# Two transformer blocks on one core: the convolution's mean one gate slab earlier, expert rows and results on ScalarE's DMA queue, half of the final sums on TensorE

## What is computed

```python
# convolution branch: mean and variance over the 512 channels of a token
u = silu(layernorm(u, ln_g, ln_b)); conv_out = u @ pw_w
logf = log_sigmoid(f_logit + fox_bf)          # forget gates, summed over time into the fox scores
merged = sigmoid(gate_c) * conv_out + sigmoid(gate_a) * attn_out
x = x + merged @ w_out
...
# experts: two per token, then the last norm
y = sum over the two chosen experts of weight * ((silu(h @ w_gate) * (h @ w_up)) @ w_down)
out = rmsnorm(x + y, norm_final_g)
```

## Time and profile before

| | |
|---|---|
| median of 3 runs | 1669.45 us (1664.61 to 1675.3) |
| profiled execution | 1670.66 us; its span 1668.9 us, 1.8 us lie around it |
| PE / PEld busy | 1468.2 us (88%) / 1156.5 us (69%) |
| DVE / ACT / POOL busy | 776.2 us (47%) / 603.4 us (36%) / 501.9 us (30%) |
| mean granted TensorE clock | 0.909 of 2.4 GHz |
| chain that ended last | PE 79%, DVE 9%, ACT 4%, issue 4%, POOL 3%, DMA 2% |

### The profile page before, as it was taken

How to read it: one execution, slowest core, us unless ns; L and a number is a source line. 1 busy time by engine, 2 the same in 40 slices (tenths; PEclk the granted TensorE clock), 3 DMA queues, 4 the chain that set the end, 5 groups by cost and what they waited for, 6 DMA issues and landing times.

```text
span 1668.9 us, 17895 instructions
## 1 busy us (share of the span) xinstructions
PE 1468.2 (88%) x7024; PEld 1156.5 (69%) x7024; DVE 776.2 (47%) x1174; ACT 603.4 (36%) x932; POOL 501.9 (30%) x202
## 2 busy tenths in 40 slices
PE   6999897799879999999968989699999889299991
PEld 4877776578668888888847867465678767277770
DVE  3358357853353533333050793334352235466654
ACT  4443244332352322223142123433333434255552
POOL 2352022000235655556334433311133520201102
PEclk9999598756899999999978999799999999599996
DMA  5232102000144544444403323100122411779964
GB/s 197 82 114 89 51 26 101 1 2 1 42 139 136 151 142 141 137 148 152 151 26 101 99 91 101 51 26 26 51 76 101 177 53 65 313 269 422 417 252 177
DMA packets 97798, 204.28 MB, mean 122 GB/s; under 512 B 6672, under 2 KB 56080, under 8 KB 91056
## 3 DMA queue, kind: packets, MB, share of 16 engines
q1 hardware_dynamic: 90512, 176.87, 31.2%
q0 software_dynamic: 7200, 26.22, 4.0%
HBM read 168.99 MB, written 34.08 MB: 122 GB/s over the span
## 4 chain that ended last, share of the span: by engine, by line
PE 79%; DVE 9%; ACT 4%; issue 4%; POOL 3%; DMA 2%; POOLq 0%; SPq 0%; DVEq 0%; ACTq 0%
PE bank L496 19%; PE bank L498 18%; PE bank L497 18%; PE bank L2618 4%; PE bank L740 3%; PE bank L759 2%; DVE rw_work L1478 2%; PE bank L750 2%; PE bank L1144 2%; PE bank L742 1%; POOL wlo L433 1%; DVE rw_beta L1476 1%; ACT whi L425 1%; PE bank L666 1%; PE bank L2585 1%
## 5 line engine op out<-in xcount | busy, mean ns | idle before, releaser
L433 POOL TENSOR_TENSOR wlo<-raw,whi 128x2048 fp32r<-128x2048 f32 (+1 forms) x84 | 382.8, 4558 | 731.9 <-ACT whi L425 731.9
L496 PE MATMUL bank<-alo,whi 128*128 128x512 f32 (+1 forms) x728 | 291.2, 400 | 18.4 <-issue 7.6
L497 PE MATMUL bank<-ahi,whi 128*128 128x512 f32 (+1 forms) x728 | 286.9, 394 | 0.0
L498 PE MATMUL bank<-ahi,wlo 128*128 128x512 f32 (+1 forms) x728 | 286.8, 394 | 0.0
L425 ACT ACTIVATE whi<-raw 128x2048 fp32r<-128x2048 f32 (+1 forms) x84 | 159.0, 1893 | 309.6 <-PE bank L498 309.6
L496 PEld LDWEIGHTS bank<-alo,whi 128*128 128x128 f32 (+1 forms) x728 | 138.7, 191 | 51.8 <-issue 14.1
L498 PEld LDWEIGHTS bank<-ahi,wlo 128*128 128x128 f32 (+1 forms) x728 | 138.6, 190 | 29.9
L497 PEld LDWEIGHTS bank<-ahi,whi 128*128 128x128 f32 (+1 forms) x728 | 138.8, 191 | 29.3 <-issue 0.7
L1889 DVE TENSOR_TENSOR ffn_relu<-ffn_relu 128x512 f32<-128x512 f32 x32 | 97.7, 3053 | 107.3 <-ACT ffn_relu L1869 107.3
L496 PE MATMUL bank<-wlo,ffn_hi 128*128 128x512 f32 x256 | 100.4, 392 | 1.3 <-POOL wlo L433 1.3
L497 PE MATMUL bank<-whi,ffn_hi 128*128 128x512 f32 x256 | 100.3, 392 | 0.0
(11 more groups left out here) (415 smaller groups left out, 2635.0 us busy)
## 6 DMA issues: line engine op xcount, KB each, us to landing
raw<-in_w_in_dram SPq DMA_DIRECT2D x18, 1024.0 KB, 5.3
expert_gate_up<-in_expert_w_gate_dram SPq DMA_DIRECT2D x17, 1024.0 KB, 10.8
expert_gate_up<-in_expert_w_up_dram SPq DMA_DIRECT2D x17, 1024.0 KB, 13.8
expert_down<-in_expert_w_down_dram SPq DMA_DIRECT2D x17, 1024.0 KB, 7.9
raw<-in_w_ffn_up_dram SPq DMA_DIRECT2D x16, 1024.0 KB, 6.7
raw<-in_w_ffn_down_dram SPq DMA_DIRECT2D x16, 1024.0 KB, 5.6
raw<-in_w_in_first_dram SPq DMA_DIRECT2D x12, 1024.0 KB, 5.4
expert_rows_dram<-zero_rows SPq DMA_DIRECT2D x23, 512.0 KB, 7.5
```

The source lines that it names most:

```text
L433: nc.gpsimd.tensor_tensor(wlo[:, n % SPLIT, 0:k * c], raw[:, n % RAW, 0:k * c], whi[:, n % SPLIT, 0:k * c].bitcast(F32), ALU.subtract).the ...
L496: nc.tensor.matmul(acc, sh, ml, start=first and i == 0, stop=False)
L497: nc.tensor.matmul(acc, sh, mh, start=False, stop=False)
L498: ins = nc.tensor.matmul(acc, sl, mh, start=False, stop=last and end)
```

## The change

It has four parts.

1. In the convolution, the mean follows the second gate slab instead of the third and the variance the third instead of the fourth. ACT's list moves with it: square root, SiLU and high parts (`act_conv_end`) stand ahead of the fourth slab's sigmoids. POOL's list has the remainder of ga.0.0 ahead of the four `u_lo`. The constant `minus8` is made by ACT instead of DVE, and DVE finishes the forget gates ahead of the reciprocal.
2. The experts' rows are read, and their results stored, by DMAs that ACT issues from its own list; POOL issues only the scatter and the gather.
3. DVE makes 8 diagonal matrices of the routing weights and then waits until POOL has issued the whole scatter (`rows_issued`, a small memset behind the 8 indirect DMAs) before it makes the first weight remainders (L2816).
4. The left 512 columns of the last sums are made on PE: the identity times `x`, plus the two diagonal matrices times the gathered rows. DVE sums the right half. ACT squares each half by itself, and DVE scales each half by itself, the left one from PSUM.

```diff
@@ pe_phase3 @@
-                for at, name, made, src in ((2, "conv_mean", conv_made, conv), (3, "conv_var", conv_dev2, conv_sq)):
+                for at, name, made, src in ((1, "conv_mean", conv_made, conv), (2, "conv_var", conv_dev2, conv_sq)):
...
-            pe.wait_ge(forget_dve, 5)
+            pe.wait_ge(forget_dve, 4)
@@ act_phase3 @@
+            nc.scalar.activation(minus8[:, :, :], ident[0:NHEAD, 0:NHEAD].unsqueeze(2).broadcast_to([NHEAD, NHEAD, P]), ACT.Copy,
+                                 scale=-float(HD) ** 0.5).then_inc(forget_act, 1)
             for i, n in enumerate(GATE_C):
-                if i == 3:
+                if i == 2:
...
+                if i == 3:
+                    act_conv_end(act)
                 for j in range(2):
                     acc = banks.take(act, f"{n}/{j}")
                     nc.scalar.activation(merged[:, 2 * i + j, :], acc[:, :], ACT.Sigmoid).then_inc(gate_sig, 1)
                 make_hi(act, act_slab, slab_no[n] + 1 + SPLIT)
@@ pool_phase3 @@
-            make_lo(pool, pool_slab, slab_no[GATE_C[3]] + 1)
+            make_lo(pool, pool_slab, slab_no[GATE_A[0]] + 1)
@@ pe_phase5 @@
+            pe_sum(pe)
+        SUM_BANKS = TURN_BANKS + GATE_UP_BANKS
+        LEFT, RIGHT = slice(0, 512), slice(512, 1024)
+        def pe_sum(pe):
+            for t in range(NT):
+                nc.tensor.matmul(SUM_BANKS[t][:, :], ident, x[:, t, LEFT], start=True, stop=False)
+            for t in range(NT):
+                pe.wait_ge(y_gathered[t], 16 * TOPK)
+                for k in range(TOPK):
+                    ins = nc.tensor.matmul(SUM_BANKS[t][:, :], diag_w[:, k, t, :], y_pair[:, t, k, LEFT], start=False, stop=k == TOPK - 1)
+                ins.then_inc(halves_summed, 1)
@@ act_phase5 @@
             act_w_hi(act, 1, 0)
+            act.wait_ge(rows_placed, 16 * NT * TOPK)
+            for i in range(2):
+                act_tile_in(act, i)
             act_x_hi(act, 0)
-            act.wait_ge(rows_placed, 16 * NT * TOPK)
+            act_tile_in(act, 2)
             for i in range(SURE):
                 if 0 < i < SURE - 1:
                     act_w_hi(act, i + 1, 0)
                 if i > 1:
                     act_y(act, i - 2)
+                    act_tile_out(act, i - 2)
                 if i:
                     act_hidden_t(act, i - 1)
                 if i < SURE - 1:
                     act_x_hi(act, i + 1)
+                    if i + 3 < SURE:
+                        act_tile_in(act, i + 3)
                     act_w_hi(act, i + 1, 1)
                 act_silu(act, i)
...
+        def act_final(act, t):
+            def after(n):
+                act.wait_ge(final_squares, 3 * t + n)
+            act.wait_ge(halves_summed, t + 1)
+            if t >= 2:
+                after(-3)
+            nc.scalar.activation(final_sq[:, t % 2, LEFT], SUM_BANKS[t][:, :], ACT.Square, accum_out=sums5[:, t:t + 1]).then_inc(final_squares, 1)
+            after(1)
+            nc.scalar.activation(sums5[:, 12 + t:13 + t], sums5[:, t:t + 1], ACT.Identity, scale=1.0 / D,
+                                 bias=const("eps")[:, 0:1]).then_inc(final_squares, 1)
+            act.wait_ge(y_sums, 2 * t + 2)
+            nc.scalar.activation(final_sq[:, t % 2, RIGHT], x[:, t, RIGHT], ACT.Square, accum_out=sums5[:, 16 + t:17 + t]).then_inc(final_squares, 1)
+            after(3)
+            nc.scalar.activation(sums5[:, 4 + t:5 + t], sums5[:, 16 + t:17 + t], ACT.Sqrt, scale=1.0 / D,
+                                 bias=sums5[:, 12 + t:13 + t]).then_inc(final_root, 1)
@@ dve_phase5 @@
             dve_route(dve, steps)
+            for k in range(TOPK):
+                for t in range(NT):
+                    steps.link(nc.vector.tensor_scalar(diag_w[:, k, t, :], ident, weight[:, k, t:t + 1], None, ALU.mult))
+            dve.wait_ge(rows_issued, 1)
             for c in range(CHUNKS):
                 dve_w_lo(dve, 0, c)
@@ dve_sum, dve_final @@
-                    nc.vector.scalar_tensor_tensor(out=x[:, t, :], in0=y_pair[:, t, k, :], scalar=weight[:, k, t:t + 1], in1=x[:, t, :],
-                                                   op0=ALU.mult, op1=ALU.add).then_inc(y_sums, 1)
+                    nc.vector.scalar_tensor_tensor(out=x[:, t, RIGHT], in0=y_pair[:, t, k, RIGHT], scalar=weight[:, k, t:t + 1],
+                                                   in1=x[:, t, RIGHT], op0=ALU.mult, op1=ALU.add).then_inc(y_sums, 1)
...
+                for part, row in ((LEFT, SUM_BANKS[t][:, :]), (RIGHT, x[:, t, RIGHT])):
+                    nc.vector.scalar_tensor_tensor(out=out_rows[:, t, part], in0=row, scalar=sums5[:, 8 + t:9 + t], in1=g[:, part],
+                                                   op0=ALU.mult, op1=ALU.mult).then_inc(final_rows, 1)
@@ tile_in, tile_out: the same steps, issued by ACT @@
+        def act_tile_out(act, i):
             s = i % 2
+            tile_done(act, y_left, i)
+            tile_done(act, y_right, i)
+            act.dma_start(y_dram[i * P:(i + 1) * P, :], y_rows[:, s, :]).then_inc(y_stored[s], 16)
@@ pool_phase5 @@
-            pool.wait_ge(rows_placed, 16 * NT * TOPK)
...
+            steps.mark(nc.gpsimd.memset(issue_mark[:, :], 0.0))
             used = later_tiles_used(pool)
```

More of the change, by code:

```diff
@@ L2127, in act_phase3 @@
                 make_hi(act, act_slab, slab_no[n] + 1 + SPLIT)
-            acc = banks.take(act, "conv_var")
-            nc.scalar.activation(crstd[:, :], acc[:, :], ACT.Sqrt, bias=const("eps")[:, 0:1]).then_inc(conv_sd, 1)
-            for m in range(KH):
-                act.wait_ge(conv_norm, m + 1)
-                nc.scalar.activation(conv[:, m, :], conv[:, m, :], ACT.Silu, bias=col("conv_ln_b_2", m)).then_inc(conv_silu, 1)
-                act.wait_ge(conv_silu, m + 1)
-                nc.scalar.activation(uhi[:, m, :], conv[:, m, :], ACT.Copy).then_inc(conv_hi, 1)
             act.wait_ge(conv_lo, KH)
@@ L2150, in act_phase3, with act_conv_end @@
                     make_hi(act, act_slab, slab_no[f"ab.{m // 4}.0"] + 1 + SPLIT)
+        def act_conv_end(act):
+            acc = banks.take(act, "conv_var")
+            nc.scalar.activation(crstd[:, :], acc[:, :], ACT.Sqrt, bias=const("eps")[:, 0:1]).then_inc(conv_sd, 1)
+            for m in range(KH):
+                act.wait_ge(conv_norm, m + 1)
+                nc.scalar.activation(conv[:, m, :], conv[:, m, :], ACT.Silu, bias=col("conv_ln_b_2", m)).then_inc(conv_silu, 1)
+                act.wait_ge(conv_silu, m + 1)
+                nc.scalar.activation(uhi[:, m, :], conv[:, m, :], ACT.Copy).then_inc(conv_hi, 1)
         def act_beside_fox(act):
@@ L2198, in dve_phase3 @@
                         before[m] = steps.mark(ins)
-            nc.vector.tensor_scalar(minus8[:, :, :], ident[0:NHEAD, 0:NHEAD].unsqueeze(2).broadcast_to([NHEAD, NHEAD, P]),
-                                    -float(HD) ** 0.5, None, ALU.mult).then_inc(forget_dve, 1)
             dve.wait_ge(forget_in, 1)
             nc.vector.tensor_scalar(forget[:, 1, :], forget[:, 0, :], 0.0, None, ALU.min).then_inc(forget_dve, 1)
-            dve.wait_ge(forget_dve, 2)
+            dve.wait_ge(forget_dve, 1)
             nc.vector.scalar_tensor_tensor(out=forget[:, 2, :], in0=forget[:, 1, :], scalar=-2.0, in1=forget[:, 0, :],
@@ L2209, in dve_phase3 @@
                 nc.vector.tensor_tensor(conv[:, m, :], conv[:, m, :], acc[:, :], ALU.subtract).then_inc(conv_dev, 1)
+            dve.wait_ge(forget_act, 3)
+            nc.vector.tensor_tensor(forget[:, 1, :], forget[:, 1, :], forget[:, 2, :], ALU.subtract).then_inc(forget_dve, 1)
+            dve.wait_ge(forget_dve, 3)
+            nc.vector.tensor_tensor_scan(forget[:, 0, :], const("ones")[0:NHEAD, 0:1].broadcast_to([NHEAD, T]), forget[:, 1, :],
+                                         0.0, ALU.mult, ALU.add).then_inc(forget_dve, 1)
             dve.wait_ge(conv_sd, 1)
@@ L2215, in dve_phase3 @@
                                                op0=ALU.mult, op1=ALU.mult).then_inc(conv_norm, 1)
-            dve.wait_ge(forget_act, 2)
-            nc.vector.tensor_tensor(forget[:, 1, :], forget[:, 1, :], forget[:, 2, :], ALU.subtract).then_inc(forget_dve, 1)
-            dve.wait_ge(forget_dve, 4)
-            nc.vector.tensor_tensor_scan(forget[:, 0, :], const("ones")[0:NHEAD, 0:1].broadcast_to([NHEAD, T]), forget[:, 1, :],
-                                         0.0, ALU.mult, ALU.add).then_inc(forget_dve, 1)
             in_turn(dve_attn(dve, steps, "fox", HD ** -0.5, const("band_causal"), masked3, peaks3, esum3,
@@ L2503, in two_blocks @@
         hidden_t = put("expert_hidden_t", [P, 2, EF])
+        issue_mark = put("issue_mark", [P, 8])
+        diag_w = put("diag_weight", [P, TOPK, NT, P])
         down_w = sb("expert_down", [P, WEIGHTS, EF // P, D], at=ring_at)
@@ L2715, in act_phase5 @@
             act_hidden_t(act, SURE - 1)
+            act_tile_out(act, SURE - 2)
             act_y(act, SURE - 1)
+            act_tile_out(act, SURE - 1)
```

(13 more changed lines are left out.)

40 lines of the change are left out of this document (13 added, 27 removed).

## The result

The changed kernel takes 1646.76 us (median of 4 runs, 1646.24 to 1652.99); beside it the kernel before took 1668.08 us (4 runs, 1664.61 to 1675.3). The ratio is 0.9868, interval 0.9844 to 0.9893. The profiled execution after is one of 1647.08 us with a span of 1645.3 us; that of before had 1670.66 and 1668.9 us.

The account below looks back on a forecast made before the run. PE, busy in 88% of the span, was taken as the bound, with gains only where it stands still: 16.0 (convolution) + 3.3 (expert head) - 0.3 (tile loop) + 4.5 (tail) = 23.5 us off 1670.7, so 1647 us, range 1641 to 1654.

Parts of the forecast that it names:

- Part 1: Convolution's end: with mean and variance one slab earlier, the first transposes of probabilities come 16.0 us sooner, bounds 14 and 18.
- The second rival: Start of the fox stage: PE's wait moves instead of going, convolution gain only 10 us, time 1653; chance 0.1.
- a clock that doesn't fall: Sign of being right: behind the fourth gate slab PE idles at most 3 us and its clock stays up.
- Part 2: Head of the expert stage: scatter issues and first rows' read gain 3.3 us, bounds 0 and 4.
- Reading tile 0: Head of the expert stage: a hardware queue instead of POOL's saves 1.0 us, bounds 0 and 1.3.
- the page weighed in the prediction: Skill page on SBUF contention at the scatter: the wait would save 0, the diagonals cost up to 2 us.
- Part 3: Tile loop: two more issues per tile on ACT, 0.85 us a tile, mostly in spare time; cost 0.3 us.
- The rival with ACT as the bound: Tile loop: ACT's issues make it slower than before, decisive from 2.75 us per issue; chance 0.04.
- Part 4, the store: Tail: the last store takes 2.6 us instead of 5.02 and issues sooner; 2.7 us saved, bounds 1.5 and 3.5.
- a last store landed in under 3 us: Sign of being right in the tail: the last store of the experts' results lands in under 3 us.
- Part 4, the final sums: Tail, from the third gathered pair: DVE's sums and scalings take 8.9 us instead of 10.7; gain 1.8 us.
- PE's clock might stay low: Tail: if PE's clock doesn't rise again, the final sums end 0.9 us slower than before instead of 1.8 faster.

Follow-up runs that it names:

- e2: The changed kernel with the convolution's edits undone (mean, variance and the lists of the other engines with them); 1660.11 us, ratio 0.9929.
- e1: The kernel before with only the edits to the convolution, the forget gates and `minus8`; 1656.71 us, ratio 0.9898.
- e4: The changed kernel with POOL's order put back, the remainder of ga.0.0 behind the four `u_lo`; 1653.19 us, ratio 0.9888.
- e6: The changed kernel with the experts' row reads and result stores back on POOL's queue; 1648.53 us, ratio 0.9871.
- e8: The changed kernel without the branches for tiles 18 to 23, unused in this routing; other routings would lose tokens; 1644.52 us, ratio 0.9852.
- e7: The changed kernel with the final sums and squares undivided on DVE and ACT, without the diagonals; 1650.68 us, ratio 0.9873.
- e5: The changed kernel without DVE's wait for the scatter's issue ahead of the first three weight remainders; 1650.36 us, ratio 0.9871.
- e11: The changed kernel with one outer branch around the six branches of the unused tiles, on all five engines; 1649.83 us, ratio 0.9859.
- e10: As e9, with ACT's high part of slab ga.0.1 also moved behind the first exponentials; 1643.73 us, ratio 0.9826.
- e9: The changed kernel with mean, variance and ACT's list one slab earlier still, remainder of ga.0.0 behind the four `u_lo` again; 1641.86 us, ratio 0.9815.
- e12: The changed kernel with the edits of e10 and e11 together; 1644.77 us, ratio 0.9832.
- e3: The kernel before with only POOL's order changed, the remainder of ga.0.0 ahead of the four `u_lo`; 1665.09 us, ratio 0.9956.

## Why the prediction was right, term by term

Predicted were 1647 us (1641 to 1654); it took 1646.76. The sum was made of 23.5 us and the profiled executions differ by 23.6. But 2.1 of these lie ahead of the first edit and are chance (see e2). From there on the kernel saved 21.4, as the medians do (21.3). So the sum was 2.1 us too large, and that the forecast still came within 0.3 us is luck: it started from an execution of 1670.66 us, 2.6 above the median of before.

*Part 1, 16.0 predicted, 16.4 measured, and alone in e1.* The mechanism held in each step that the text named: the root came out at 1044.08, or 1046.16 with the 2.08 us by which that trace ran ahead (forecast 1046.1), and was used by a reciprocal of 3.36 us; POOL's remainder was off the chain; ACT's list, not POOL's, ended last; PE waited 1.93 us where the text had about 2. e4 shows the edit of POOL's list in it, 5.2 us. One step was missing: the text gave PE's wait to ga.0.0's remainder alone and counted the forget gates as free, while before the change they held up the first scores until 1067.16. The second rival, that the wait moves (10 us), fell.

*What part 1 left out: the clock behind the short wait.* The text counted 2 us of waiting and named a clock that doesn't fall as a sign of being right. It fell. Seven profiled executions have that same wait of 1.93 us, and their half clock lasts 0 us (e6, e8), 3.4 (after, e7), 10 (e5) and 14 (e1, e11), by windows of 1 us, up to 0.7 us of it still beside the wait. Why it lasts so differently is open.

How much of it the median gets is chance: the four times of the kernel after are 1646.24, 1646.44, 1647.08 and 1652.99. A long dip (a stretch at half clock) would put an execution into the upper group, and the profiled ones fit that, but they are all that was seen of it: those of e1, e5 and e11 are 1658.58, 1652.80 and 1653.16 us, at or within 0.2 us of the top of their four, those of e6 and e8 1646.55 and 1644.21, in the lower half. e7 doesn't fit as well: a short dip, and still 363.7 us up to the scatter and 1651.28 in all, so the stretches behind it have chances of their own. The spread of e10, 7.0 us without any wait or dip in its profiled execution, says so too. With the wait at 0.6 us or gone (e9, e10, e12) none of three executions dips there.

*Part 2, 3.3 predicted, 2.7 measured.* The issues gave 2.66 us of span where the text had 2.9, and the DMA took 0.56 back (landing 4.76 against 4.20 us), which leaves 2.1 where 2.3 was taken. Reading tile 0, from the end of its wait on, gave 0.65 instead of 1.0. e6 splits the 2.7: 2.3 us come with POOL's queue kept (before to e6; 0.2 of them from a shorter read) and 0.4 with the other queue (e6 to after). That the remainders slow the issues is what the page weighed in the prediction spoke against: "SBUF — State Buffer" of the Trainium skill, section "Who interferes with whom", infers that a tensor_tensor leaves descriptor making alone, and says that a tensor_scalar can shut POOL out. The traces have it the other way about, 1.9 us beside the tensor_tensor and 0.95 beside the diagonals, and the measurement decides. By "DMA: Bandwidth & Descriptors" of the Trainium skill, section "Specifications", the difference of the two queues would be about 0.4 us (an estimate from its first-byte times); here the trace agrees for the read: from the scatter's landing to the read's it is 3.71 us in e6 and 3.28 after. Only 0.16 of that is in the transfer's own row (3.42 against 3.26).

*Part 3, 0.3 lost predicted, 0.3 gained measured*, both within what two executions differ. An issue takes 0.33 us, PE is busy in 120 of 120 us, and e6 with POOL's queue has the same loop (174.17 against 174.5; all fourteen kernels lie between 174.17 and 175.39). The rival with ACT as the bound would have needed issues of 2.75 us.

*Part 4, the store: 2.7 predicted, 0.9 measured.* This is the term that was mis-sized, and its sign of being right, a last store landed in under 3 us, did not come. The text took the 2.6 us of the output store for a store that ran 5.02 us, and gave the whole difference to the queue. In the kernel after the store still took 4.26 us. ACT issued it 0.4 us sooner, but POOL's first gather came 0.3 us later behind the landing. The queue is worth about 0.6 us (means above). Another 1.7 us hang on something else at that place: with ACT's queue and six branches the store took 4.00 to 5.06 us in seven kernels, with one branch 4.47 (e11) and 2.62 (e12), and without branches 2.61 (e8). The engines pass the skipped branches just then and fetch instructions by DMA; without the branches (e8) the instruction packets and the slow store are both gone. But e11 and e12, with one branch each and as many instruction packets, differ by 1.9 us, and e4 has 2 packets and the longest store. What sets it is open.

*Part 4, the final sums: 1.8 predicted, 1.6 measured*, and 1.5 by e7. DVE's 8.9 us were 9.06. That PE's clock might stay low there, which the text weighed, didn't come about: behind the identity products the clock is 1.00 from 1624 to 1642, where it was 0.50 before, and a tile's half sum takes PE 1.98 us. The identity products themselves started 4.48 us late because of the branches and took 5.28 us instead of 3.4, the first of them at half clock, but still ended ahead of the first gathered tile.

## What to carry to other kernels

When PE waits for a chain of small steps, look first for a whole slab of products that can be put between the chain's start and its use, and then at the order of the list of the slowest engine in it: here the first, with the earlier forget gates, was worth 11 to 12 us and the second 4 to 5. A wait of 2 us that is left in front of a busy PE cost 2 to 8 us in the seven profiled executions, since the half clock behind it varied.

Moving the chain one more slab ahead took 4.9 us off the median (e9 against the kernel after; the ratios to their own runs of before are 0.9815 and 0.9868, and their intervals don't meet), of which the profiled executions show 1.3 at the fox stage and 1.6 in the next stretch.

Price a transfer by the row at its own place: the same 512 KB took 2.6 us at one place and 5 at another, and the queue was the smaller part of that. A store's or an issue's length from one execution is not enough for a term under 1 us.

## What was not expected of the hardware

- The same wait of 1.93 us of PE was followed by 0, 3.4, 10 or 14 us at 1.2 GHz in seven executions.
- Indirect DMA issues on POOL took 1.9 us beside a 128x2048 tensor_tensor of DVE and 0.95 us beside 128x128 tensor_scalars, in the same execution (e5).
- Six skipped branches cost PE 4.48 us in the kernel after (4.17 to 6.41 in seven kernels), a single one around them 0.85 us (e11) and 2.11 us (e12).
- Faster issues came with a longer last landing: 4.76 to 4.79 us behind issues every 1.26 us (ten kernels), against 4.19 to 4.23 (before, e1, e3) and 3.78 us (e5) where three had been slow.
